# Page compression in ten chunks over four slots, one of them the weight ring, and block scores with stationary keys in four column groups

## What is computed

```python
def compress_blocks(rows, pe, w1, w2):          # rows: b, l, heads, 64
    z = rows.reshape(b, l // 64, 64, g, d) + pe
    z = transpose(z, (0, 1, 3, 2, 4)).reshape(b, l // 64, g, 64 * d)
    return silu(z @ w1) @ w2
...
kc = compress_blocks(rows_k, cmp_pe[0], cmp_w1[0], cmp_w2[0])
vc = compress_blocks(rows_v, cmp_pe[1], cmp_w1[1], cmp_w2[1])
s_c = einsum('btgrd,bngd->bgrtn', qg, kc) * scale + bias_c
p_c = masked_softmax(s_c, dist_c >= 0)
```

## Time and profile before

| | us |
|---|---|
| median of 3 runs (lowest, highest) | 1663.26 (1659.61, 1663.38) |
| the profiled execution | 1662.27 |
| its span | 1660.6 |
| projection, to | 141.7 |
| compression stage | 141.7 to 255.8 |
| TensorE busy over the span | 1573.7 (95%) |
| DMA over the span | 238.37 MB, 144 GB/s |

### The profile page before, as it was taken

How to read it: one execution, slowest core, us unless ns; L and a number is a source line. 1 busy time by engine, 2 the same in 40 slices (tenths; PEclk the granted TensorE clock), 3 DMA queues, 4 the chain that set the end, 5 groups by cost and what they waited for, 6 DMA issues and landing times. The chain is left out here.

```text
span 1660.6 us, 38408 instructions
## 1 busy us (share of the span) xinstructions
PE 1573.7 (95%) x15550; PEld 1466.9 (88%) x15550; DVE 811.4 (49%) x1353; ACT 555.6 (33%) x1059; POOL 566.4 (34%) x514
## 2 busy tenths in 40 slices
PE   7997898899989999999998899999899999999996
PEld 7997894566689999999998889999799999999995
DVE  4331126666647444343137677786547344443145
ACT  4120105565555222222235433334345222222242
POOL 0002104677614444343004334342024443443013
PEclk9999789999999999999999999999899999999998
DMA  6855887877350222223243142433141222223242
GB/s 214 316 177 175 306 336 311 305 266 242 116 200 32 90 89 91 96 92 118 91 145 131 64 129 78 154 107 130 61 138 39 77 99 91 88 93 110 100 157 87
DMA packets 87377, 238.37 MB, mean 144 GB/s; under 512 B 18333, under 2 KB 21071, under 8 KB 85793
## 3 DMA queue, kind: packets, MB, share of 16 engines
q1 hardware_dynamic: 81528, 221.41, 38.5%
q0 software_dynamic: 3392, 11.02, 1.9%
q10 hardware_dynamic: 2314, 3.96, 0.7%
HBM read 217.81 MB, written 23.77 MB: 145 GB/s over the span
## 5 line engine op out<-in xcount | busy, mean ns | idle before, releaser
L867 DVE TENSOR_TENSOR layer_w_lo<-ring,layer_w_hi 128x1024 fp32r<-128x1024 f32 (+1 forms) x136 | 223.0, 1640 | 257.9 <-ACT layer_w_hi L746 257.9
L1025 PE MATMUL layer_ps<-layer_x_hi,layer_w_hi 128*128 128x260 f32 x1312 | 268.8, 284 | 5.1 <-DVE layer_w_lo L867 2.7
L1025 PE MATMUL layer_ps<-layer_x_hi,layer_w_lo 128*128 128x260 f32 x1312 | 267.3, 283 | 0.0
L1025 PE MATMUL layer_ps<-layer_x_lo,layer_w_hi 128*128 128x260 f32 x1312 | 266.8, 283 | 0.0
L746 ACT ACTIVATE layer_w_hi<-ring 128x1024 fp32r<-128x1024 f32 (+1 forms) x136 | 158.7, 1169 | 206.8 <-PE layer_ps L1025 206.8
L1025 PE MATMUL layer_ps<-layer_h_lo,layer_w_hi 128*128 128x260 f32 x960 | 217.6, 287 | 8.8 <-DVE layer_h_lo L876 8.8
L1025 PEld LDWEIGHTS layer_ps<-layer_x_hi,layer_w_hi 128*128 128x128 f32 x1312 | 203.8, 189 | 6.6 <-DVE layer_w_lo L867 2.9
L1025 PEld LDWEIGHTS layer_ps<-layer_x_hi,layer_w_lo 128*128 128x128 f32 x1312 | 203.7, 189 | 0.0
L1025 PEld LDWEIGHTS layer_ps<-layer_x_lo,layer_w_hi 128*128 128x128 f32 x1312 | 203.1, 188 | 0.3
L1025 PE MATMUL layer_ps<-layer_h_hi,layer_w_hi 128*128 128x260 f32 x704 | 172.8, 286 | 4.8 <-DVE layer_w_lo L867 4.8
L1025 PE MATMUL layer_ps<-layer_h_hi,layer_w_lo 128*128 128x260 f32 x704 | 170.2, 282 | 0.0
(11 more groups left out here) (338 smaller groups left out, 2936.1 us busy)
## 6 DMA issues: line engine op xcount, KB each, us to landing
ring<-in_w_gu SPq DMA_DIRECT2D x88, 512.0 KB, 3.2
ring<-in_w_down SPq DMA_DIRECT2D x48, 704.0 KB, 4.1
arena<-in_cache_cmp SPq DMA_DIRECT2D x68, 256.0 KB, 6.1
ring<-in_hgrn_w_in SPq DMA_DIRECT2D x32, 512.0 KB, 6.0
ring<-in_nsa_w_in SPq DMA_DIRECT2D x21, 512.0 KB, 4.9
kv_slot<-in_slc_kv SPq DMA_DIRECT2D x32, 256.0 KB, 4.7
arena<-in_slc_kv SPq DMA_DIRECT2D x32, 256.0 KB, 4.8
X<-in_slc_kv SPq DMA_DIRECT2D x32, 256.0 KB, 4.0
```

Of the source, the lines that this page charges most:

```text
L867: dve.tensor_tensor(self.w_lo[slot][:, 0:kcs * P], c.ring[:, s, 0:kcs * P], self.w_hi[slot][:, 0:kcs * P].bitcast(F32), ALU.subtract).then ...
L1025: mm = pe.matmul(bank[:, h, 0:TH], wt[slot][:, a], xt[:, x, COLS[h]], start=start and part == 0, stop=stop and part == 2)
```

## The change

- **Chunks.** Ten chunks with a table of slot and pages. There are four slots: the halves of `arena` (0, 1), `c.ring` (2, 11 pages), `kv_slot` (3). Chunks of 16 pages are 0, 1, 5, 6; of 11 pages 2, 3, 7, 8; of 10 pages 4 and 9. The ring's first 11 pages are loaded by SyncE late in the projection (`store_last`), each group of them when the weight tile in its part of the ring has been cut.
- **Stores.** `kv_out` is stored unit by unit in the projection: five units beside weight tiles, three units behind, and seven in `store_last`.
- **Places.** What lay in the ring lies elsewhere: `z` in the sample bias tile, the scores in `kcT`, the block bias in `block_probsT`, `w2` and `pe_in` in `vcS`, the rest in a new small tile and in `rstd`.
- **Waits.** VectorE's pair copies wait for nothing; only the copies of `pe_in` wait for its load, and `w2` has a semaphore of its own, awaited by TensorE. SyncE loads both ahead of all pages.
- **Scores.** The keys are stationary (32 columns, 16 of them zero), the queries move, 512 columns at a time. Four products go to four column groups of one bank, twice. ScalarE copies both banks to SBUF, TensorE turns eight 128 x 128 tiles, VectorE scales and adds the bias in two halves.

```diff
+CHUNKS = ((0, 16), (1, 16), (2, 11), (3, 11), (0, 10), (1, 16), (3, 16), (2, 11), (0, 11), (1, 10))
...
                 if s < rest:
                     load_tile(sp, c, w, s, loops * RING + s, kcs)
-                    sp.wait_ge(c.lo_cut[s], base_done[s] + loops + 1)
+                    if behind is None:
+                        sp.wait_ge(c.lo_cut[s], base_done[s] + loops + 1)
+                elif behind is not None:
+                    behind(sp, s)
...
+            if behind is not None:
+                sp.wait_ge(c.lo_cut[0], base_done[0] + loops + 1)
+                behind(sp, 0)
...
         def _(sp):
-            sp.dma_start(pe_in, d["cmp_pe"]).then_inc(small, 16)
-            load_chunk(sp, 2, 0)
-            sp.dma_start(w2, d["cmp_w2"]).then_inc(small, 16)
+            sp.dma_start(pe_in, d["cmp_pe"]).then_inc(pe_loaded, 16)
+            sp.dma_start(w2, d["cmp_w2"]).then_inc(w2_loaded, 16)
+            sp.dma_start(mask, d["head_mask"]).then_inc(head_mask, 16)
+            load_chunk(sp, 3, 0)
+            load_chunk(sp, 4, 0)
             sp.dma_start(oh, d["onehot_rows"][:, 1]).then_inc(onehots, 16)
-            sp.dma_start(mask, d["head_mask"]).then_inc(head_mask, 16)
-            sp.dma_start(at.bias[0:N_BUCKETS + 1, :], d["onehot_sample"]).then_inc(onehots, 16)
+            load_chunk(sp, 5, 0)
+            load_chunk(sp, 6, 0)
+            sp.wait_ge(prompt_done, 1)
+            sp.dma_start(at.bias[0:N_BUCKETS + 1, :], d["onehot_sample"]).then_inc(far_onehots, 16)
...
             def block_scores():
 
+                pe.wait_ge(kc_ready, 1)
+                pe.wait_ge(v_copied, 1)
+                for r in range(2):
+                    for q in range(4):
+                        mm = pe.matmul(b[r][32 * q:32 * q + 32, :], kcBD[:, r, :], c.XW[:, 4 * r + q, 0:SEQ],
+                                       start=True, stop=True)
+                    mm.then_inc(score_rows, 1)
+
+            def turn_scores():
+
                 pe.wait_ge(bias_out, 1)
-                pe.wait_ge(kc_ready, 1)
-                for i in range(TILES):
-                    for u in range(8):
-                        col = (i * 8 + u) * 16
-                        mm = pe.matmul(b[2][:, col:col + 16], c.XW[:, u, i * P:(i + 1) * P],
-                                       kcBD[:, u // REP].rearrange("p g n -> p (g n)"), start=True, stop=True)
-                mm.then_inc(scores, 1)
+                pe.wait_ge(tok_out, 2)
+                for r in range(2):
+                    pe.wait_ge(score_rows_out, r + 1)
+                    for i in range(TILES):
+                        mm = pe.transpose(b[2 + r][:, i * P:(i + 1) * P], score_row[:, r, i * P:(i + 1) * P], c.ident[:, :])
+                    mm.then_inc(scores, 1)
...
-            for j in range(4, 6):
-                far(j)
...
         def _(dve):
             own = Seq(dve, own_done)
-            dve.wait_ge(small, 32)
...
+            own(dve.memset(kcBD[:, :, :], 0.0))
+            dve.wait_ge(pe_loaded, 16)
+            for kv in range(2):
+                for g2 in range(2):
                     own(dve.tensor_copy(z[:, kv, :, g2, PR], pe_in[:, kv, :]))
...
+            def ring_pages(sp, first, count):
+
+                for x in range(first, first + count):
+                    j = first_page(2) + x
+                    page = sp.value_load(c.pages[0:1, j:j + 1], min_val=0, max_val=POOL - 1)
+                    sp.dma_start(c.ring[:, :, :].rearrange("p r n -> p (r n)")[:, x * 512:(x + 1) * 512],
+                                 d["cache_cmp"][bass.ds(page, 1)].rearrange("o p n -> p (o n)")).then_inc(ring_in, 16)
+
+            def store_last(sp, slot):
+
+                pages, tiles = (((0, 2), (18, 19)), ((2, 3), (13, 14, 15)), ((5, 3), (16,)), ((8, 3), (17,)))[slot]
+                ring_pages(sp, *pages)
+                for tile in tiles:
+                    store_unit(sp, tile)
```

More of the change, by code:

```diff
@@ L55 @@
 HEAD_TILES = 3
+STORE_BEHIND = 3
+STORED_BESIDE = 5
 class Seq:
@@ L135, in repeat, with linear @@
             yield i
-def linear(c, name, w, n_units, subs, kcs, src, evac, nxt, scale=None, beside=None, norm=None, early=None, late=None, work=None, unrolled=False, first=None, start=0, opening=None):
+def linear(c, name, w, n_units, subs, kcs, src, evac, nxt, scale=None, beside=None, norm=None, early=None, late=None, work=None, unrolled=False, first=None, start=0, opening=None, behind=None):
     nc = c.nc
@@ L1153, with first_page @@
 PAGES_A_CHUNK = 16
+CHUNKS = ((0, 16), (1, 16), (2, 11), (3, 11), (0, 10), (1, 16), (3, 16), (2, 11), (0, 11), (1, 10))
+HALF_CHUNKS = 5
+EARLY_CHUNKS = 3
+def first_page(g):
+    return sum(n for _, n in CHUNKS[:g])
 def carve(flat, at, *shape):
@@ L1297, in compress, with share, brought @@
             ("scores", "shifted", "exp", "probs", "turned", "turned_out", "values_laid_out")]
-        kv_saved = sem("kv_saved")
         block = ctx.enter_context(nc.Block())
-        flat = [at.arena[:, 0:CH * 512], at.arena[:, CH * 512:2 * CH * 512], at.rows_c[:, :]]
-        slot = lambda x: flat[x].rearrange("p (g n) -> p g n", g=CH)
-        taken = lambda s, last: len(range(s, last + 1, 3))
-        SHARE = ((0, 9), (9, 7))
+        arena_slot = PAGES_A_CHUNK * 512
+        flat = [at.arena[:, 0:arena_slot], at.arena[:, arena_slot:2 * arena_slot], ring, at.rows_c[:, :]]
+        rows = lambda g: flat[CHUNKS[g][0]].rearrange("p (g n) -> p g n", n=512)
+        taken = lambda s, last: sum(slot == s for slot, _ in CHUNKS[:last + 1])
+        def share(g, who):
+            n = CHUNKS[g][1]
+            cut = (9 * n + 8) // 16
+            return (0, cut) if who == 0 else (cut, n - cut)
+        def brought(who, g):
+            return sum(share(x, who)[1] for x in range(EARLY_CHUNKS, g + 1) if CHUNKS[x][0] == CHUNKS[g][0])
         FAR = [(j * 512, 512) for j in range(5)] + [(PAST + WIN, NBLK + 1)]
@@ L1433, in _ @@
             chunk(5)
+            chunk(6)
+            block_scores()
             values(0, b[5])
```

161 lines of the change are left out of this document (91 added, 70 removed).

## The result

The changed kernel took 1645.31 us (median of 4 runs, 1643.78 to 1646.96), the kernel before beside it 1663.32 us: a ratio of 0.9894, 95% interval 0.9877 to 0.9911, so 18.0 us less. That is inside the range of 1633 to 1648 and 6.3 us above the forecast of 1639. The profiled execution took 1646.96 us (span 1645.3), the longest of the four.

The account below looks back on a forecast made before the run. TensorE's nearly closed string of work was taken to bound the compression stage; -14.6 - 3.4 + 0.6 - 7.6 + 1.3 = -23.7 us took 1662.27 to 1638.6, stated as 1639 (forecast 1636 to 1641, range 1633 to 1648).

Parts of the forecast that it names:

- The removed wait: Before the prompt's products: VectorE's pair copies no longer wait for w2's load, so TensorE's idle time goes, -14.6 us.
- the prompt at full clock: Prompt's products directly behind chunk 1 run at full instead of half clock, 3.4 instead of 6.85 us: -3.4 us.
- the cost of short chunks: Ten chunks instead of eight: 5.0 us for 11 pages, 4.6 for 10; +0.6 us in sum, slow pieces included.
- the scores: Prompt's block scores: 16 records of 512 columns in 2.0 us; with turns and copies 3.15 replace 10.76, -7.6 us.
- the turns: Eight transposes of the scores on TensorE at 0.127 us each, 1.0 us, counted within the scores' -7.6.
- the end: Between last chunk and second products: sample-bias products no longer cover ScalarE's table load and first SiLU, +1.3 us.
- The rival by which weights bind short chunks: All six short chunks take 6.85 us each, bound by weight loads the clock doesn't change: +11.9, 1650.5 us; chance 0.06.
- The rival of a clock that stays low: Short chunks don't bring the clock back after the prompt: +35.5, 1674 us; chance 0.03, and 0.03 for a partial form.
- Column groups overlap at 512 columns: Score products in four column groups take 2.0 us; the rival without overlap had 7.6, total 1644, chance 0.04.
- The pages: Page loads of the compression stage arrive before TensorE wants them, chunk 6 tightest at 186 against 189: no wait, 0.
- up to +5 if chunk 6 comes late: Rival: chunk 6's pages, started only at 172, bring a wait of 1 to 5 us, total 1640 to 1645; chance 0.12.
- The slow pieces: Four slow pieces of 1.6 us kept among the chunks, after prompt, bias, values with turned scores, and transposes: 6.4 us.

Follow-up runs that it names:

- f2: Changed kernel with kv_out stored in one 3.1 MB transfer behind chunk 5's pages and no unit stores in the projection: 1652.3 us, ratio 0.9936 to before.
- f1: Changed kernel with chunk 2's 11 ring pages loaded at the start of the compression stage instead of in the projection: 1655.6 us, ratio 0.9947 to before.
- b1: Kernel before with one line moved, so that SyncE issues w2 ahead of its nine pages: 1664.6 us, ratio 0.9981 to before.
- d1: Changed kernel with the old block scores, 32 products of 16 columns, without score-row copies or turns: 1659.4 us, ratio 0.9955 to before.
- e3: Changed kernel with chunks 6 and 7 swapped, kv_slot's chunk cut to 11 pages, chunk 8 given 16, last two sample-bias products behind chunk 9: 1642.4 us.
- c1: Changed kernel with w2 issued behind SyncE's pages of chunk 3 and the pair copies waiting for it again: 1657.1 us, ratio 0.9948 to before.
- a3: The changed kernel run again, unchanged, beside later edits: 1643.3 us, ratio 0.9885 to before.
- e1: Changed kernel with chunks 6 and 7 in the other order, the ring's 11 pages ahead of kv_slot's 16: 1645.7 us, ratio 0.9889 to before.
- f3: The e3 kernel with a one-column SiLU run by ScalarE before it waits for chunk 9: 1641.0 us, ratio 0.9861 to before.

## Why the prediction was right, and where it wasn't

**Right, with its size.** The removed wait (in the changed kernel), the prompt at full clock, the cost of short chunks, the scores, the turns and the end: each within 1.3 us in the first profile, as the table of terms shows. Chunks 7 and 8 take 5.00 us at the full clock, 39 ns a record, as said, and chunk 9, of 10 pages, 4.64.

- The rival by which weights bind short chunks is out. The prompt's 128 records take 3.70 us at the full clock, 28.9 ns each, each with a load of 64 columns. The Trainium skill (TensorE: Matmul & The Clock Gate, on LDWEIGHTS) gives 53 ns for such a load; by it, one after the other, they would take 6.8 us. What the profile showed before, 53.5 ns a record, was the half clock.
- The rival of a clock that stays low is out: it came back in each slow chunk.
- Column groups overlap at 512 columns: 1.86 us for 16 records, 116 ns each.
- The attention keeps its length: from its first product to the first of the recurrence 687.2 and 686.7 us pass in the profiles of before, 687.7, 686.8 and 687.0 in those of the changed kernel.

**The term that failed is "The pages", whose sum was 0 and whose bound "up to +5 if chunk 6 comes late".** This rival, with a chance of 0.12, is what happened, in every profile of the changed kernel: 2.5, 5.5 and 1.8 us of wait, and in two of the three a slow chunk behind. The step put the slot free at "about 172", the landing at 186 and the chunk's turn at 189. In the first profile these were 173.5, 193.4 and 190.9: the landing was 7.4 us late, the turn 1.9.

- 1.5 us is the slot. The stage began 1.0 us later and chunks 2 and 3 lost 0.25 and 1.21 us in waits for "issue", while the slow piece of 1.6 behind the prompt, which the sum kept, did not come.
- 1.6 us is the rate: 4.2 MB take 12.6 us at the 333 GB/s that the 16 us ahead of chunk 6 moved, and 11 at the 380 of the rows.
- Some 4 us are what the step left out: that the two queues share the transfers. GpSimd's seven pages, the last issued at 181.57, had landed by 187.3. SyncE's last was issued at 183.42 and took 9.9 us, twice the median of its nine. GpSimd's pages for chunk 7, issued from 182.71 on, landed in 6.5 to 8.1 us, so three of them were there first. The one-hots of the samples, issued right behind at 183.79, are the other suspect: 188 to 192 us moved 262 GB/s at full share, and in before the 4 us that begin 4.7 us behind the same load moved 239 (158 to 162 us). No run moved that load or shifted pages from SyncE to GpSimd, so how these 4 us divide stays open.

**A sentence that was wrong with no effect on the sum:** that the store among the chunks "goes with nothing gained, as no one waited for it". No one did as long as TensorE stood 14.6 us for w2. With that wait gone, f2 shows 9.0 us for the store and f1 12.3 for the early pages, and b1 shows that in the kernel before, with neither, the removed wait is worth 2.5. So the prediction had the sum right in part by luck: both moves were in the change, and the sum counts a gain for neither. On the one line alone its terms (14.6 + 3.4) would have missed by 15 us. It never laid the bytes of the stage, 25.2 MB of pages and 3.1 of the store, beside the shorter time.

**Two slips in its arithmetic, neither with weight.** SyncE's nine issues of 9.06 us start 1.09 us apart, the last being 0.34 long, not 1.01: 470 GB/s with GpSimd's and not 490, still more than was moved. And 1638.6 with 1.0 added is 1639.6, where it says 1639.

**The slow pieces.** Four were kept, with the sum's own warning that they were unknown. In the first profile two came, 3.2 us of the 6.4: behind the bias (6.2 for 4.6) and behind the wait for chunk 6. The waits for "issue" in chunks 2 and 3, 1.5 us, were in no term. The stretch with the scores gave none, in any of the profiles with column groups, and two with the old scores (d1). So beside 8 us of products the old scores cost some 4 of clock, which the sum had not counted as gain.

**Between stage and total.** 21.2 us in the stage, on the mean of the profiles, became 18.0 to 20.6 in the medians. The rest is of the size by which the recurrence differs between executions, and stays open below that.

## What to carry to other kernels

A wait is worth what it covers last: before pricing its removal, take it away on paper and lay the bytes of the stage beside the new, shorter time, by the rates of long full stretches (327 to 401 GB/s here). Edits that seem free (a store moved, loads begun in an idle stage) may be what lets the priced one pay; one run with the priced line alone tells. And where a chunk comes over two queues, look at each queue's last page: what stood ahead in the same queue delayed it (the store in f2), and what the other queue issued later landed first. Spreading what is wanted next more evenly over both would be the next thing to try; no run here did.

## What the runs showed of the hardware

- **A wait and the clock behind it.** The chunk that follows a wait for its pages kept the full level behind waits of 0.5, 1.2, 1.8 and 3.2 us (e3, c1, a3, e1) and was slow behind 2.5, 3.3, 3.4, 3.6, 4.3, 5.5, 7.7, 8.4 and 13.3 us: 8.7 to 9.6 us long instead of 7.2, at a mean granted clock of 0.74 to 0.81 instead of 1.00. That 3.2 kept the level and 2.5 lost it shows that the length of the wait alone doesn't decide. (Behind 0.19 us in the first profile of before the chunk is slow too, but there the clock had fallen in the scores ahead.) The price hardly grows with the wait: one of 2.5 us cost 4.2 in all, one of 13.3 us 15.1.
- **Waits for "issue" at fixed places.** TensorE stops after 50 or 51 records of a chunk for 0.25 to 1.48 us: in chunk 3 in every profile of the changed kernel and its edits but c1's, in chunk 2 in seven of them, while the transfers are full (share 1.02 from 168 to 172 us in the first). Whether its instructions wait behind pages was not tried.
- **Two queues, one supply.** With the transfers full, the pages that GpSimd issued later landed ahead of SyncE's in f2, b1 and the changed kernel (the rows above), and 4 us at a DMA share of 1.04 moved anything from 239 GB/s (before, 158 to 162) to 385 (before, 222 to 226). A full share does not tell the rate.
- **The clock can fall around chunk 9** when it follows turns and sample-bias products directly (5.8, 6.1, 7.1 us in e1, e3, f3, at 0.78, 0.74 and 0.63), though the chunk behind the same stretch of the changed kernel kept the full level in all three profiles (5.0). What tells the two apart is open.
